# The last rows of a routed-expert kernel: final gain folded into the squares, a tile handed to GpSimd, scatters swapped

## The reference, cut to what matters

```python
def rms(x, g):
    xf = x.astype(jnp.float32)
    y = xf * lax.rsqrt(jnp.mean(xf * xf, axis=-1, keepdims=True) + EPS)
    return (y * g.astype(jnp.float32)).astype(x.dtype)

x = x + gate2 * ec_moe(h2, ...)      # each expert adds its result to the rows that it chose
y_prompt = rms(xc, g_final)
y_sample = rms(xl, g_final)
```

## Time and profile before

| | us |
|---|---|
| median of 3 runs | 3317.91 |
| lowest and highest of them | 3317.41, 3318.12 |
| the profiled execution | 3315.78 |
| its span, first to last instruction | 3313.7 |
| granted TensorE clock, mean over the span | 0.991 |
| TensorE busy (matmuls) | 3235.8 |
| VectorE busy | 2121.0 |
| ScalarE busy | 1391.5 |
| GpSimd busy | 358.4 |

### The profile page before, as it was taken

How to read it: one execution, slowest core, us unless ns; L and a number is a source line. 1 busy time by engine, 2 the same in 40 slices (tenths; PEclk the granted TensorE clock), 3 DMA queues, 4 the chain that set the end, 5 groups by cost and what they waited for, 6 DMA issues and landing times. The chain is left out here.

```text
span 3313.7 us, 39738 instructions
## 1 busy us (share of the span) xinstructions
PE 3235.8 (98%) x15947; PEld 2506.7 (76%) x15947; DVE 2121.0 (64%) x1875; ACT 1391.5 (42%) x1271; POOL 358.4 (11%) x445
## 2 busy tenths in 40 slices
PE   7999999999999999999999999969999999999997
PEld 4888888888888999998888888746666666666664
DVE  4355565565552777773233243279999999999997
ACT  3221222221212445452121222247777777777775
POOL 0020010020000000001101112100111111111102
PEclk9999999999999999999999999979999999999999
DMA  9575555485553110125353455379999999999999
GB/s 398 215 230 176 202 178 175 159 271 197 186 187 119 38 48 34 40 101 207 133 172 135 151 172 191 127 256 373 388 398 396 388 384 387 396 393 385 389 391 338
DMA packets 143918, 787.25 MB, mean 238 GB/s; under 512 B 19888, under 2 KB 30672, under 8 KB 63936
## 3 DMA queue, kind: packets, MB, share of 16 engines
q1 hardware_dynamic: 101344, 666.40, 52.2%
q0 software_dynamic: 42448, 119.03, 12.1%
HBM read 718.11 MB, written 67.25 MB: 237 GB/s over the span
## 5 line engine op out<-in xcount | busy, mean ns | idle before, releaser
L102 DVE TENSOR_TENSOR w_lo<-w_stage,w_hi 128x2048 fp32r<-128x2048 f32 x379 | 863.5, 2287 | 95.9 <-ACT w_hi L97 94.7
L97 ACT ACTIVATE w_hi<-w_stage 128x2048 fp32r<-128x2048 f32 x379 | 727.4, 1920 | 299.7 <-PE e_ps L109 299.7
L107 PE MATMUL i_ps<-w_hi,hT_hi 128*128 128x512 f32 (+1 forms) x1440 | 563.0, 391 | 0.1
L109 PE MATMUL i_ps<-w_hi,hT_lo 128*128 128x512 f32 (+1 forms) x1440 | 554.7, 385 | 0.0
L108 PE MATMUL i_ps<-w_lo,hT_hi 128*128 128x512 f32 (+1 forms) x1440 | 554.5, 385 | 0.0
L107 PE MATMUL e_ps<-w_hi,xgT_hi 128*80 128x512 f32 x1024 | 404.3, 395 | 0.0
L108 PE MATMUL e_ps<-w_lo,xgT_hi 128*80 128x512 f32 x1024 | 403.2, 394 | 0.0
L109 PE MATMUL e_ps<-w_hi,xgT_lo 128*80 128x512 f32 x1024 | 400.6, 391 | 0.0
L599 DVE TENSOR_TENSOR w_lo<-w_raw,w_hi 128x2048 fp32r<-128x2048 f32 (+1 forms) x72 | 161.7, 2246 | 345.6 <-ACT w_hi L458 345.6
L107 PE MATMUL p_ps<-w_hi,xT_hi 128*128 128x512 f32 x960 | 377.9, 394 | 1.4 <-DVEq L1841 1.4
L109 PE MATMUL p_ps<-w_hi,xT_lo 128*128 128x512 f32 x960 | 374.1, 390 | 0.0
(11 more groups left out here) (365 smaller groups left out, 4490.9 us busy)
## 6 DMA issues: line engine op xcount, KB each, us to landing
w_stage<-in_w_e SPq DMA_DIRECT2D x384, 1024.0 KB, 7.4
w_stage<-in_w_ada SPq DMA_DIRECT2D x96, 1024.0 KB, 7.1
w_raw<-in_w_in SPq DMA_DIRECT2D x64, 1024.0 KB, 5.0
w_stage<-in_w_o_gm SPq DMA_DIRECT2D x16, 1024.0 KB, 7.4
w_stage<-in_w_o_mla SPq DMA_DIRECT2D x16, 1024.0 KB, 5.1
w_stage<-in_w_out SPq DMA_DIRECT2D x16, 1024.0 KB, 5.0
acts<-evacuated POOLq DMA_DIRECT2D x60, 256.0 KB, 4.4
side<-acts POOLq DMA_DIRECT2D x40, 256.0 KB, 5.5
```

What stands on the lines that cost most here:

```text
L97: act.activation(dst, src, ACT.Copy).then_inc(st.hi, 1)
L102: dve.tensor_tensor(dst, src, hi.bitcast(F32), ALU.subtract).then_inc(st.split, 1)
L107: pe.matmul(out, x_hi, w_hi, start=first, stop=False)
L109: return pe.matmul(out, x_lo, w_hi, start=False, stop=last)
```

## The change

- GpSimd norms tile 1 (`F_POOL`), in four instructions on halves of 128x1024: two multiplies by the row's factor (one tensor read), then two by `g_final` (two tensors read). They stand in its queue behind the stores of tile 0 and before those of tile 1. VectorE still computes the tile's mean and reciprocal, not its two multiplies.
- The last rows: while ScalarE sums the squares of `xg`, VectorE writes `y = xg * g_final` (`l_gained`). When the factor is known, ScalarE multiplies the left half of `y` by it and VectorE the right half. The scatters read `y`.
- The right half of the last expert's result is taken in two parts of 512 columns. TensorE finishes its last piece column half by column half, so that the first part is ready two matmuls earlier. On VectorE both parts now stand behind tile 4's multiplies, where `out(LAST, 1)` and `l_add(1)` stood before them; `l_add(0)` stands behind tile 0 and not before it.
- The scatter of the 64 latent rows is issued before that of the 16 context rows.

```diff
+    F_POOL = 1
+    last_part = lambda p: slice((0, D // 2, D // 2 + NC)[p], (D // 2, D // 2 + NC, D)[p])
 # GpSimd
-            for t in range(TT):
-                pool.wait_ge(f_ok, 2 * t + 2)
+            def store_y(t):
                 dst = O["y_prompt"][0] if t == 0 else O["y_sample"][0, bass.ts(t - 1, P), :]
                 for h in range(2):
                     pool.dma_start(dst[:, bass.ts(h, D // 2)], f_x[t][h][:]).then_inc(f_out[t], 16)
+
+            pool.wait_ge(f_ok, 2)
+            store_y(0)
+            pool.wait_ge(g_in, 16)
+            pool.wait_ge(f_inv, F_POOL + 1)
+            for h in range(2):
+                x = f_x[F_POOL][h][:]
+                pool.tensor_scalar(x, x, fst[:, 4, F_POOL:F_POOL + 1], None, ALU.mult).then_inc(f_pool, 1)
+            for h in range(2):
+                x = f_x[F_POOL][h][:]
+                pool.wait_ge(f_pool, h + 1)
+                pool.tensor_tensor(x, x, g_final[:, bass.ts(h, D // 2)], ALU.mult).then_inc(f_pool, 1)
+            pool.wait_ge(f_pool, 4)
+            store_y(F_POOL)
+            for t in range(F_POOL + 1, TT):
+                pool.wait_ge(f_ok, 2 * t)
+                store_y(t)
             pool.wait_ge(rows_y_ok, 2)
             pool.wait_ge(l_ok, 2)
-            pool.wait_ge(f_out[0], 32)
-            pool.indirect_dma_start(out=O["y_prompt"][0], ..., in_=xg[CAP_LAT:SLOTS, 0:D], ...)
             for t in range(1, TT):
                 pool.wait_ge(f_out[t], 32)
-            pool.indirect_dma_start(out=O["y_sample"][0], ..., in_=xg[0:CAP_LAT, 0:D], ...)
+            pool.indirect_dma_start(out=O["y_sample"][0], ..., in_=y[0:CAP_LAT, :], ...)
+            pool.wait_ge(f_out[0], 32)
+            pool.indirect_dma_start(out=O["y_prompt"][0], ..., in_=y[CAP_LAT:SLOTS, :], ...)
 # ScalarE
-            l_square(0)
-            l_square(1)
+            for p in range(3):
+                l_square(p)
             act.wait_ge(l_var, 1)
             act.activation(rst[:, 3:4], rst[:, 2:3], ACT.Sqrt).then_inc(l_std, 1)
+            act.wait_ge(l_inv, 1)
+            act.wait_ge(l_gain, 1)
+            c = last_part(0)
+            act.activation(y[:, c], y[:, c], ACT.Copy, scale=rst[:, 4:5]).then_inc(l_ok, 1)
 # VectorE
+            def last_out_part(p):
+                dve.wait_ge(*((l_half, 2) if p == 1 else (s.used, NW + n0 + 4 * PB)))
+                c = last_part(p)
+                dve.scalar_tensor_tensor(y[:, c], pair[3][0:SLOTS, p - 1, :], cur_gate[:], gate2[:, c], ALU.mult, ALU.mult).then_inc(y_ev, 1)
+
+            def l_gained(p):
+                dve.wait_ge(l_x, p + 1)
+                c = last_part(p)
+                dve.tensor_tensor(y[:, c], xg[:, c], g_final[0:SLOTS, c], ALU.mult).then_inc(l_gain, 1)
             f_variance(0)
+            f_inverse(0)
+            f_normal(0)
+            f_variance(F_POOL)
+            f_inverse(F_POOL)
             l_add(0)
-            for t in range(TT):
-                if t == TT - 1:
-                    out(LAST, 1, n0 + 4 * PB)
-                    l_add(1)
+            l_gained(0)
+            for t in range(F_POOL + 1, TT):
+                f_variance(t)
+                f_inverse(t)
                 f_normal(t)
-                if t + 1 < TT:
-                    f_variance(t + 1)
+            for p in range(1, 3):
+                last_out_part(p)
+                l_add(p)
+                if p == 1:
+                    l_gained(p)
             dve.wait_ge(l_sq, 2)
             dve.tensor_tensor(rst[:, 2:3], rst[:, 0:1], rst[:, 1:2], ALU.add).then_inc(l_sum, 1)
+            l_gained(2)
+            dve.wait_ge(l_sq, 3)
             dve.wait_ge(l_sum, 1)
+            dve.tensor_tensor(rst[:, 2:3], rst[:, 2:3], rst[:, 5:6], ALU.add).then_inc(l_sum, 1)
             ...
-            for h in range(2):
-                c = bass.ts(h, D // 2)
-                dve.scalar_tensor_tensor(xg[:, c], xg[:, c], rst[:, 4:5], g_final[0:SLOTS, c], ALU.mult, ALU.mult).then_inc(l_ok, 1)
+            dve.wait_ge(l_gain, 3)
+            c = bass.ts(1, D // 2)
+            dve.tensor_scalar(y[:, c], y[:, c], rst[:, 4:5], None, ALU.mult).then_inc(l_ok, 1)
 # TensorE, down_plain
-                for jj in range(2):
+                ends = j == 4 * PB - 1
+                for jj, cc in ((0, 0), (1, 0), (0, 1), (1, 1)) if ends else ((0, 0), (0, 1), (1, 0), (1, 1)):
                     ...
+                    if ends and (jj, cc) == (1, 0):
+                        ins.then_inc(l_half, 1)
```

More of the change, by code:

```diff
@@ L2041, in phase_experts @@
     inv_rows = m.new("r_inv_rows", [P, TT, 16], F32)
-    fst, rst = m.new("f_stats", [P, 5, TT], F32), m.new("last_stats", [SLOTS, 5], F32)
+    fst, rst = m.new("f_stats", [P, 5, TT], F32), m.new("last_stats", [SLOTS, 6], F32)
     assert m.at <= M.phase_at + 2 * X_END + X_END // 4 * 3 + 6144
@@ L2069, in phase_experts @@
             *(sem(f"f_{n}") for n in ("sq", "sum", "var", "std", "inv", "ok", "rows")), M.pool_sem("last_out"))
-        l_x, l_sq, l_sum, l_var, l_std, l_inv, l_ok, l_warm, l_half, l_raw = (sem(f"last_{n}") for n in ("x", "sq", "sum", "var", "std", "inv", "ok", "warm", "half", "raw"))
+        l_x, l_sq, l_sum, l_var, l_std, l_inv, l_ok, l_half, l_raw, l_gain, f_pool = (
+            sem(f"last_{n}") for n in ("x", "sq", "sum", "var", "std", "inv", "ok", "half", "raw", "gain", "f_pool"))
         clear_finished(nc, M)
@@ L2187, in _ @@
                     pool.dma_start(dst[:, bass.ts(h, D // 2)], f_x[t][h][:]).then_inc(f_out[t], 16)
+            pool.wait_ge(f_ok, 2)
[14 more added lines that the diff above has]
+                store_y(t)
             pool.wait_ge(rows_y_ok, 2)
             pool.wait_ge(l_ok, 2)
-            pool.wait_ge(f_out[0], 32)
-            pool.indirect_dma_start(out=O["y_prompt"][0], out_offset=bass.IndirectOffsetOnAxis(ap=rows_ctx[:, 0:1], axis=0),
-                                    in_=xg[CAP_LAT:SLOTS, 0:D], in_offset=None).then_inc(last_out, 16)
             for t in range(1, TT):
@@ L2195, in _ @@
             pool.indirect_dma_start(out=O["y_sample"][0], out_offset=bass.IndirectOffsetOnAxis(ap=rows_lat[:, 0:1], axis=0),
-                                    in_=xg[0:CAP_LAT, 0:D], in_offset=None).then_inc(last_out, 16)
+                                    in_=y[0:CAP_LAT, :], in_offset=None).then_inc(last_out, 16)
+            pool.wait_ge(f_out[0], 32)
+            pool.indirect_dma_start(out=O["y_prompt"][0], out_offset=bass.IndirectOffsetOnAxis(ap=rows_ctx[:, 0:1], axis=0),
+                                    in_=y[CAP_LAT:SLOTS, :], in_offset=None).then_inc(last_out, 16)
             pool.wait_ge(last_out, 32)
@@ L2284, in f_root, with l_square @@
                 act.activation(fst[:, 3, t:t + 1], fst[:, 2, t:t + 1], ACT.Sqrt).then_inc(f_std, 1)
[L2286 to L2289, removed]
+            def l_square(p):
+                act.wait_ge(l_x, p + 1)
+                if p:
+                    act.wait_ge(l_sq, p)
                 else:
                     act.wait_ge(f_sq, 2 * TT)
-                act.activation(pair[0][0:SLOTS], xg[:, bass.ts(h, D // 2)].rearrange("p (c n) -> p c n", c=2), ACT.Square,
-                               accum_out=rst[:, h:h + 1]).then_inc(l_sq, 1)
+                c, own = last_part(p), slice(0, 1 if p else 2)
+                act.activation(pair[0][0:SLOTS, own, :], xg[:, c].rearrange("p (c n) -> p c n", n=NC), ACT.Square,
+                               accum_out=rst[:, (0, 1, 5)[p]:(0, 1, 5)[p] + 1]).then_inc(l_sq, 1)
             n0 = NP * (LAST - 1) + N0
@@ L2303, in _ @@
                 if j == 8:
-                    act.activation(rst[:, 3:4], M.ident[0:SLOTS, 0:1], ACT.Sqrt).then_inc(l_warm, 1)
+                    act.activation(rst[:, 3:4], M.ident[0:SLOTS, 0:1], ACT.Sqrt).then_inc(l_std, 1)
                 if j == 22:
@@ L2316, in _ @@
                     f_squares(t + 1)
-            l_square(0)
-            l_square(1)
+            for p in range(3):
+                l_square(p)
             act.wait_ge(l_var, 1)
-            act.wait_ge(l_warm, 1)
+            act.wait_ge(l_std, 1)
             act.activation(rst[:, 3:4], rst[:, 2:3], ACT.Sqrt).then_inc(l_std, 1)
+            act.wait_ge(l_inv, 1)
+            act.wait_ge(l_gain, 1)
+            c = last_part(0)
+            act.activation(y[:, c], y[:, c], ACT.Copy, scale=rst[:, 4:5]).then_inc(l_ok, 1)
         @block.vector
@@ L2462, in f_variance, with f_inverse, f_normal @@
                 dve.tensor_scalar(fst[:, 2, t:t + 1], fst[:, 2, t:t + 1], 1.0 / D, EPS, ALU.mult, ALU.add).then_inc(f_var, 1)
-            def f_normal(t):
+            def f_inverse(t):
                 dve.wait_ge(f_std, t + 1)
                 dve.reciprocal(fst[:, 4, t:t + 1], fst[:, 3, t:t + 1]).then_inc(f_inv, 1)
+            def f_normal(t):
                 dve.wait_ge(f_inv, t + 1)
@@ L2471, in f_normal, with l_add @@
```

(27 more changed lines are left out.)

4 lines of the change are left out of this document (2 added, 2 removed).

## The result

| | before | changed |
|---|---|---|
| median of 17 runs, us | 3317.91 | 3324.14 |
| lowest and highest | 3315.24, 3320.93 | 3320.76, 3327.64 |
| span of the profiled execution | 3313.7 | 3322.8 |
| ratio of the times | | 1.0017 (95% interval 1.0011 to 1.0024) |

The change makes the kernel 6.2 us slower by the medians (3.6 to 8.0 by the interval of the ratio). The forecast was 5.0 us slower, in a range that holds the measured time.

A forecast was written before the change was run, and what follows sets the result against it. VectorE's queue was taken to bound the tail. Its shortening (−0.3), the scatters (−1.2) and GpSimd's exclusion (+6.6) summed to +5.1 us on the span, forecast as 3322.9 us against the median 3317.91; range 3316.0 to 3325.5.

The forecast's parts named there:

- VectorE's queue is the bound of the tail: After TensorE's last matmul: VectorE works without a pause over 0.3 us until 3305.03, so its queue bounds the tail.
- The queue without interference: VectorE's tail, GpSimd not disturbing it: last result at 3304.7 against 3305.03, 0.3 us earlier.
- rival D: VectorE's tail: the 2.40 us saved goes on l_gained and exposed squares; already in the sum (−0.3), no chance of its own.
- Exclusion, and VectorE pays: Tile norms: GpSimd and VectorE shut each other out, VectorE is stopped, 6.6 us late; forecast case, chance 0.66.
- the walk: Tail instructions followed in order, whoever asks first going first: tile 2 ends 6.6 us late through GpSimd's four instructions.
- the upper bound of 10: GpSimd's four multiplies: durations sum to 7.3 us, bounds 4.0 and 10; a sum outside these would show the prediction wrong.
- Its own rule: Tail total: the four GpSimd durations, less 0.7 of small steps beside, less 1.5 gained without interference; +5.1 us.
- rival C: GpSimd's four multiplies take over 8.8 us, so the kernel is measurably slower, from +6.6 us on; chance 0.14.
- the copy of 189 ns: Earlier trace: a GpSimd copy, given as 80x1, that met no one; compared with one taking 2.25 us beside a VectorE split.
- stay ahead of VectorE: Stores of tiles 1 to 4: GpSimd issues them from 3298 on, 1.05 us each, and stays ahead of VectorE.
- Rival B: VectorE isn't stopped by GpSimd: 3316.4 us, up to 3318.5 if GpSimd's store queue holds the last scatter; chance 0.18.
- The scatters, −1.2: Closing: issuing the large scatter first and the small one last saves 1.2 us, between 0 and 1.3.

The follow-up runs named there:

- n8: Kernel before with each tile's sum and mean moved between the two multiplies of the tile ahead; median 3317.56 us against 3318.29, ratio 0.9996.
- n6: Changed kernel with GpSimd's four multiplies replaced by eight memsets of 128x1024, tile 1's norm left out; one execution, 3321.75 us.
- n1: Changed kernel with tile 1's two multiplies back on VectorE, GpSimd only issuing; median 3320.57 us, ratio to the kernel before 1.0008.
- n9: Changed kernel with GpSimd's two multiplies by the gain replaced by two more one-tensor multiplies; one execution, 3325.50 us.
- n3: Kernel before with four added GpSimd multiplies of the same kinds and sizes on a spare buffer; one execution, span 3320.8 us.
- n5: Changed kernel with the tiles' stores issued from SP's queue; median 3322.73 us, ratio to the kernel before 1.0013.
- n2: Kernel before with GpSimd norming tile 1 and nothing else of the change; median 3324.64 us, ratio 1.0022.
- n4: Kernel before with the two scatters swapped and nothing else; median 3318.90 us, ratio 1.0003.

## Why the prediction was right, and where it was not

- *VectorE's queue is the bound of the tail.* Right for the kernel before: n8 shortens nothing else, and T to L and the end follow. In the changed kernel it is so up to L only; behind L the stores set the end. TensorE's new order brought nothing: VectorE takes the first part up at 3306.72, 9.1 us after the last matmul.
- *The queue without interference.* The prediction walked from 3283.6 to 3304.7, 21.1 us from T to L; n6 measures 21.41. Part of the difference is ScalarE's last multiply, 1.15 where it was priced at 1.00. The gain of 0.8 us from moving l_add(0) back came out as 0.3 (T lies 11.25 us ahead of the last matmul's end, 10.91 before), since VectorE then waited 0.35 for the squares of tile 0. So the last rows' new path costs 23.79 − 20.66 = 3.1 us from T to L (n1), more than the 2.40 that GpSimd takes off VectorE: from T on, the change would be 0.75 slower even without interference. This is rival D, and it held. Where the prediction had −0.3 for this part, it came out as +0.4 (0.75 less the 0.3 by which T is earlier in the changed kernel).
- *Exclusion, and VectorE pays.* Right in kind: it is what makes L late. It is not what alone decided the sign, since the stores would have set nearly the same end without it (0.3 us sooner by the estimate at n9). The stretch of 5.2 stands where the walk had 6.6. The walk took the order of events nearly as it was, but the lengths wrongly: one-tensor multiplies last 2.9 us, not 1.25, and stop VectorE for 0.8; two-tensor ones 2.36, near the 2.4 taken, and stop it for 2.14 and 1.43. The sum of the four's durations alone is 5.9 + 4.8 = 10.7 (n3), above the upper bound of 10, which the prediction had named as a sign of being wrong. Its own rule, the sum less 0.7 less 1.5, would then have given +8.5, more than rival C's threshold of +6.6. Measured were 6.2: the rule charged the whole duration to VectorE. Nor did most of the stretch fall before tile 2 was done, as the walk had it: tile 2's multiplies began 7.1 us after T (6.3 without interference), and 3.6 of the 5.2 came behind them. The prediction's evidence had a slip, too: the copy of 189 ns in the earlier trace rows is one of 16x16, not of 80x1. The conclusion stands all the same: the copy of 80x1 whole numbers that follows the slow one at 3222.53 takes 0.17 us.
- The Trainium skill ("SBUF — State Buffer", who interferes with whom) has the exclusion for the whole instruction. The two-tensor rows agree (stopped until 3299.01 and 3301.31, GpSimd's own ends), and so does n6, where writes alone stop nothing, as the page says. The one-tensor rows don't: 0.8 of 2.9 us. The measurement decides.
- *GpSimd's stores "stay ahead of VectorE".* Wrong, and the step of the prediction that failed. It had GpSimd's arithmetic end at 3298, 14.4 us after T, which is near the 14.9 measured. But it priced the stores behind it by their issue, 1.05 a tile, not by the time that four tiles of 1 MB need on the DMA engines. From 3301.61 to 3314.12 they took 12.5 us. That put 1.1 us more between L and the scatter; n5 takes it away. n6 and n9 show that the change had two losses side by side: with VectorE free, the stores alone would have set an end nearly as late. Rival B had seen this way to a later end ("its queue of stores holds the last scatter"), but gave it no more than 2.1 us.
- *The scatters, −1.2.* Wrong; 0 was its stated worst case. In nine of the ten kernels of the table, all but n2, 7.7 to 7.9 us lie between the first scatter and E, whichever goes first. The small one lands in 4.5 behind the large one and in 3.2 ahead of it. And its wait moved: n4's trace shows +1.3 from L to E.
- In sum: forecast for the tail −0.3 + 6.6 − 1.2 = +5.1. Measured from the last matmul's end: T 0.3 earlier, T to L +6.0, L to E +1.1, together +6.7; by medians +6.2. The errors of VectorE's part (forecast +6.3, measured +5.6) and of the closing (−1.2 against +1.1) have opposite signs, and so have those inside VectorE's part (−0.3 against +0.4 without interference, 6.6 against 5.2 of stretch). So the total is closer than its terms, and that it is so close is luck. The sum also adds the stretch and the closing as if one came after the other; in the changed kernel the stretch and the stores ran side by side.
- The prediction called 6.6 us "about what a measurement of this kernel can tell from no change". The interval of the result reaches 2.2 us to either side.

## What to carry to other kernels

Before giving work to GpSimd to relieve VectorE, look at what VectorE does meanwhile: a two-tensor GpSimd instruction took from VectorE up to 2.2 us of its own 2.4, and two of them (3.6 us in the changed kernel, 4.1 in n2) cost more than the 2.4 of work taken away. One-tensor ones that had their turn in VectorE's pauses cost it nearly nothing (n9). And an engine that issues the stores must not compute ahead of them: their transfers, not their issue, set when the last one is home. When two losses run side by side, as here VectorE's stretch and the burst of stores, taking away one of them may gain little. Of two transfers that end a kernel, the one with fewer waits goes first (n4's trace; its times don't show it).

## What the hardware showed

- A GpSimd multiply of 128x1024 f32 by a number per row took 2.84 to 2.94 us with VectorE idle, one by a second tensor 2.36 us where nothing held it up (n3). The one that reads less is the slower.
- The first stopped VectorE for 0.80 to 0.86 us (changed kernel, n2, n9), or 0.04 to 0.05 where VectorE was between two tiles (n9). The second stopped it for 2.14 and 1.43 (changed kernel), 4.12 for two (n2) and 2.16 (n3). A GpSimd memset of the same size took 0.97 us and stopped it not at all (n6).
- It goes the other way as well: a two-tensor multiply that was due while a VectorE multiply ran took 2.77 us (changed kernel) and 3.31 (n2) where it takes 2.36, and a one-tensor one 3.27 (n9) and 3.66 (n5) where it takes 2.9.
- Four tiles of 1 MB, stored in one burst from GpSimd's queue, were home 12.4 to 12.5 us after the first issue in four kernels (changed, n2, n6, n9).
- A VectorE instruction on one number per row (0.15 us) took 2.29 when it had to wait for a two-tensor GpSimd instruction: the length of such a row says nothing about its work.
